# Splitting each tap of a 31-tap causal depthwise convolution on VectorE into two half-width instructions

## The reference

```python
ua, ub = jnp.split(cu, 2, axis=-1)
u = ua * jax.nn.sigmoid(ub)
u = causal_depthwise_conv(u, conv_dw_w, conv_dw_b)      # 31 taps, one filter for each channel
u = jax.nn.silu(layer_norm(u, conv_ln_g, conv_ln_b))
y_conv = u @ conv_w_proj
return (gate_a * y_gla + gate_b * y_conv) @ w_mix_out
```

## Time and profile before

| | us |
|---|---|
| median of 3 runs | 2579.86 (2576.95 to 2581.59) |
| the profiled execution | 2576.95 |
| its span, first to last instruction | 2575.2 |
| PE busy | 2496.0 (97%) |
| DVE busy | 1163.2 (45%) |
| line 1366, 240 instructions | 414.4 busy, 36.3 idle before them |

### The profile page before, as it was taken

One profiled execution on the slowest core, in us unless ns is written; L12 is line 12 of the kernel. 1 busy time (PEld: TensorE's weight loads), 2 busy tenths in 40 slices (PEclk: granted clock), 3 DMA queues, 4 the chain that ended last, 5 costly groups with the idle time before them and its releaser, 6 DMA issues. The chain is left out here.

```text
span 2575.2 us, 29372 instructions
## 1 busy us (share of the span) xinstructions
PE 2496.0 (97%) x11636; PEld 2081.1 (81%) x11636; DVE 1163.2 (45%) x1259; ACT 643.9 (25%) x823; POOL 721.7 (28%) x319
## 2 busy tenths in 40 slices
PE   7999999999999999999999986999899999999997
PEld 6888888888878889889879864888688888888886
DVE  4222222222253498598597597643622222222224
ACT  4111111111164233233333221411611111111112
POOL 2222222222262223233232273221622222222223
PEclk9999999999999999999999987999999999999999
DMA  5111111111132022132032044423511111111103
GB/s 175 50 49 49 49 49 49 49 49 49 57 123 66 25 84 60 38 99 58 25 99 74 27 162 139 159 89 114 178 50 48 44 47 45 45 49 49 49 33 114
DMA packets 189182, 184.49 MB, mean 72 GB/s; under 512 B 5813, under 2 KB 158883, under 8 KB 189091
## 3 DMA queue, kind: packets, MB, share of 16 engines
q1 hardware_dynamic: 182563, 170.67, 21.8%
q10 hardware_dynamic: 6528, 12.58, 1.3%
HBM read 150.72 MB, written 32.51 MB: 71 GB/s over the span
## 5 line engine op out<-in xcount | busy, mean ns | idle before, releaser
L442 PE MATMUL PU<-XH,w_h 128*128 128x512 f32 x2448 | 964.1, 394 | 12.2 <-POOL XL L1615 6.8
L444 PE MATMUL PU<-XH,w_l 128*128 128x512 f32 x2448 | 956.7, 391 | 0.0
L443 PE MATMUL PU<-XL,w_h 128*128 128x512 f32 x2448 | 956.5, 391 | 0.0
L1492 POOL TENSOR_TENSOR w_l<-w_raw,w_h 128x2048 fp32r<-128x2048 f32 (+1 forms) x83 | 389.9, 4697 | 1027.0 <-ACT w_h L750 1026.9
L442 PEld LDWEIGHTS PU<-XH,w_h 128*128 128x128 f32 x2448 | 462.3, 189 | 116.9 <-POOL XL L1615 11.4
L444 PEld LDWEIGHTS PU<-XH,w_l 128*128 128x128 f32 x2448 | 461.9, 189 | 96.9
L443 PEld LDWEIGHTS PU<-XL,w_h 128*128 128x128 f32 x2448 | 462.6, 189 | 95.7 <-issue 0.8
L1366 DVE SCALAR_TENSOR_TENSOR acc<-ub,cw,acc 128x1024 f32<-128x1024 f32 x240 | 414.4, 1727 | 36.3 <-DVE acc L1366 3.2
L1167 DVE TENSOR_TENSOR hf<-PU,sgt 128x512 f32<-128x512 f32 x88 | 60.8, 691 | 814.7 <-ACT sgt L817 814.7
L492 PE MATMUL PG<-o_h,H 128*128 128x512 f32 x832 | 325.5, 391 | 4.4 <-DVE FACC L1159 4.1
L493 PE MATMUL PG<-o_l,H 128*128 128x512 f32 x832 | 324.5, 390 | 0.0
(11 more groups left out here) (147 smaller groups left out, 1591.1 us busy)
## 6 DMA issues: line engine op xcount, KB each, us to landing
w_raw<-in_ffn_w_in SPq DMA_DIRECT2D x88, 512.0 KB, 5.0
w_raw<-in_w_mix_in SPq DMA_DIRECT2D x50, 512.0 KB, 5.1
o_raw<-in_ffn_w_out SPq DMA_DIRECT2D x44, 512.0 KB, 3.5
x_d<-FACC SPq DMA_DIRECT2D x16, 512.0 KB, 2.9
gate_d<-tmp ACTq DMA_DIRECT2D x16, 512.0 KB, 3.3
gt<-gate_d SPq DMA_DIRECT2D x16, 512.0 KB, 5.4
xt<-x_d SPq DMA_DIRECT2D x12, 512.0 KB, 4.2
FACC<-in_x SPq DMA_DIRECT2D x8, 512.0 KB, 6.3
```

The source lines that it names most:

```text
L442: pe.matmul(dst, hi(k), xh(k), start=(n == 0), stop=False)
L443: pe.matmul(dst, hi(k), xl(k), start=False, stop=False)
L444: last = pe.matmul(dst, lo(k), xh(k), start=False, stop=(n == KT - 1))
L1492: PT(w_l[:, par, :, c], w_raw[:, par, :, c], w_h[:, par, :, c], ALU.subtract).then_inc(w_lo, 1)
```

## The change

Each tap becomes two instructions, one for tokens 0 to 511 and one for tokens 512 to 1023 of `acc`. They alternate, and each waits not for the instruction just before it but for the one before that, which is the one that wrote its half (both halves read only `ub` beside it). There are 62 instructions in a convolution instead of 31, 61 of them count on `conv_step` and the last on `conv_free`. Nothing else changes.

```diff
-                    per = TAPS - 1
-                    o = acc[:, a, :]
+                    per = 2 * TAPS - 1
                     for w in range(TAPS):
-                        src = ub[:, a, w:w + SEQ]
-                        tap = cw[:, ds(8 * w + a + 2 * h, 1)]
-                        if w == 0:
-                            op = TS(o, src, tap, cols[:, ds(V_CB + a + 2 * h, 1)], ALU.mult, ALU.add)
-                        else:
-                            dve.wait_ge(conv_step, per * (2 * h + a) + w)
-                            op = STT(o, src, tap, o, ALU.mult, ALU.add)
-                        op.then_inc(conv_step if w < per else conv_free, 1)
+                        for half in range(2):
+                            n = 2 * w + half
+                            o = acc[:, a, half * HALF:(half + 1) * HALF]
+                            src = ub[:, a, half * HALF + w:half * HALF + w + HALF]
+                            tap = cw[:, ds(8 * w + a + 2 * h, 1)]
+                            if w == 0:
+                                op = TS(o, src, tap, cols[:, ds(V_CB + a + 2 * h, 1)], ALU.mult, ALU.add)
+                            else:
+                                dve.wait_ge(conv_step, per * (2 * h + a) + n - 1)
+                                op = STT(o, src, tap, o, ALU.mult, ALU.add)
+                            op.then_inc(conv_step if n < per else conv_free, 1)
```

## The result

The changed kernel takes 2686.61 us (median of 4 runs, 2685.11 to 2687.89) against 2580.43 for the kernel before; the ratio is 1.0411, 95% interval 1.0396 to 1.0425. That is 107 us above the forecast, and on the side of the rival "POOL is starved", to which I gave 0.05 and for which I had worked out 2760. The span of the profiled execution grew from 2575.2 to 2682.3 us, by 107.1.

The account below looks back on a forecast made before the run. PE bounds the kernel, busy 97%; DVE counts only through the last turn's two convolutions before `mean()`. There 6.2 us saved and 6.0 lost make -0.2, so 2579.7 us against the median of 2579.86; range 2572 to 2592.

Parts of the forecast that it names:

- POOL is starved: Rival, all convolutions: without gaps DVE wins every time and POOL waits for a convolution's end; +180 us, 2760; chance 0.05.
- the disturbed part: Last turn's two convolutions: 26 meetings with POOL's instructions, each costing 0.23 us more than now, 6.0 us lost.
- the rival without overlap: Rival, all convolutions: halves start only when the pipe is empty, 0.78 us each; +23.5 us, 2603; chance 0.10.
- the 25.3 us before `mean()`: PE's idle time in the last turn, waiting for DVE's chain; forecast to grow to over 30 us.
- the 0.145 us of waiting: Ahead of each dependent tap: wait and address arithmetic, said to fit in the 0.58 us since the needed half finished.
- The disturbed period: Half taps alternating with POOL's 512-element instructions: one every 1.67 us, against 2.215 for whole taps.
- Gain and loss on the last turn's chain: Last turn's two convolutions: 6.2 us saved undisturbed, 6.0 lost in meetings with POOL, together -0.2 us.
- The restart at `mean()`: Last turn: PE restarts 15.5 us after the last tap, so any shift up to 25 us earlier, or later, moves it.
- slack: First three turns: 4.9 us before PE needs DVE's work, so shorter convolutions there are worth nothing.

Follow-up runs that it names:

- experiment 2: The changed kernel, but the first half of every fourth tap waits for the half just before it, all others overlapping: 2578.2 us, ratio 0.9989.
- experiment 6: Kernel before the change with whole taps adding in turn into two accumulators, each waiting for the tap before the last, no gaps: 2668.1 us, ratio 1.0336.
- experiment 9: The changed kernel with a gap (a wait for the half just before) at every eighth tap, three in a convolution: 2583.2 us, ratio 1.0009.
- experiment 4: The changed kernel with only conv(1) of each turn in halves, conv(0) in whole taps as before: 2654.8 us, ratio 1.029.
- experiment 5: The changed kernel with a one-column DVE memset ahead of every fourth tap and no added wait: 2579.2 us, ratio 0.9998.
- experiment 8: The kernel before the change, with POOL's five layer norm additions and following low part held back until the last convolution ended: 2571.8 us, ratio 0.9958.
- experiment 1: The changed kernel, but each half waits for the half just before it, so the gap is back: 2648.2 us, ratio 1.0265.
- experiment 7: Whole taps with two accumulators, as in experiment 6, but every fourth tap waits for the tap just before it: 2572.5 us, ratio 0.9959.

## Why the prediction was wrong

**The step that failed** is the argument against the rival "POOL is starved": that POOL's instructions stand in a row without gaps and the taps get in between each two, and that "A port that lets the waiting one in that way should do so the other way too." The rows were right and the symmetry was not. In these traces DVE gets in between POOL's instructions every time. POOL gets in between DVE's only at the beginning of an unbroken row, up to the seventh instruction or 4.5 us; when it asks later, it waits for a break (experiments 2, 6, 9). The one exception is the 57th half of each conv(1) of the change. Those rows of before could not show it, since each tap had a gap ahead of it. The same error sits in "the disturbed part", which counts 26 meetings in which POOL takes its turn. The prediction says that no row has this combination, but only beside the rival without overlap; it gave starvation 0.05 on the strength of that symmetry alone.

**The rival's price** was 20 us for each conv(0) and 26 for each conv(1), four times. Measured: 23.5 for conv(0), as POOL's queue had the instruction on `ub` ahead of line 1501's; 9 to 12 for conv(1), where late address arithmetic let POOL in, and 20 to 24 where it did not (experiment 4). It left out that the 25.3 us before `mean()` would pay for a part. So its 180 us were 107.

**Right in size.** A half starts every 0.66 us (39.85 us for 60) and lasts 0.747; conv(0) takes 40.8 us (40.6); the 0.145 us of waiting fit behind the overlap. The disturbed period is 1.70 us (1.67), the conv(1) that meets POOL at its start 76.3 (76.6). Gain and loss on the last turn's chain nearly cancel where POOL is let in: from conv(0) to `mean()` experiment 2 takes 147.0 us and experiment 5 144.5, against 145.1, and both totals stand within 0.2% of the kernel before. As they have breaks or memsets that the change has not, they bear the sum out without being the kernel that it was made for.

**Right in kind.** The restart at `mean()` is the last tap's end plus a fixed way, and POOL's instructions under that convolution lengthen it by their own time (experiment 8). The convolutions of the first three turns have slack: experiment 2 shortens conv(0) by 1.1 us there, and PE has no wait less. How much a longer pair costs was not as simple as pair less slack (experiment 1).

**The two pages.** The Trainium skill's page "VectorE: DVE Perf Modes", section "The DRAIN you can't avoid", as the prediction read it, would make the half taps slower on DVE; the section also says that a next instruction that is not held starts earlier, which the prediction left out. The trace agrees with the latter: they are faster there, 40.8 us against the 43.7 worked out for whole taps. The number of instructions, which the page's rules advise to keep low, was not the reason for the loss (experiments 1 and 6). The Trainium skill's "SBUF — State Buffer", "Who interferes with whom", says that a DVE instruction with two SBUF inputs contends with a GpSimd instruction that reads SBUF, and that one with at most one, outside the modes that use two ports, does not: the memset of experiment 5 and line 1376 in experiment 9 agree. It also says that the loser blocks for the whole instruction; here it blocked for a whole row of them, 27 to 34 us.

**What stays open.** Why POOL is let in after up to 6 unbroken halves and not after 8 is not shown. The order and the times of the address arithmetic between the halves are the same in both cases. Whether the limit is a count of instructions or a time is open too: no halves asked at 7, no whole taps between 3 and 6, and no request came between 4.5 and 5.5 us. Why the late address arithmetic let POOL in is not shown either, nor whether an instruction with one SBUF input always breaks a row: tap 0 of the conv(1) behind the two of line 1376, which has one, was held up until POOL had ended, 2.47 us for 0.53.

## What to carry to other kernels

A gap on an engine can be somebody else's turn. Before a dependency stall is taken off a row of VectorE instructions with two SBUF inputs, look for GpSimd work that has to run under it, and leave a break every few instructions: here one memset of one column in every four taps cost 0.02 us each and was worth 107 us in all. And look at what the second engine's instructions do to the chain: moving six of GpSimd's from under the last convolution was worth 0.4% by itself (experiment 8), as much as the shorter convolutions were (experiment 7), and both together 0.7% to 0.8%.

## What the runs showed of the hardware

- An overlapped row of DVE instructions with two SBUF inputs held up a GpSimd instruction of 1.3 us for 32.0 us (512 elements), 27.4 (1024), and one of 2.4 us for 34.0.
- In rows without a break it got in when at most 6 of them had started before the running one (4.5 us), and after 7 or more (5.5 us or more) in no case but one: the same half of four convolutions, ahead of which DVE's address arithmetic was 0.35 us late.
- A DVE memset of 128 x 1, with no gap before or after it, let it in; so did a gap of 0.145 us, and an instruction with one input in PSUM and one in SBUF.
- Once the two alternate, they went on doing so as long as GpSimd had work queued: half taps every 1.70 us with 512-element GpSimd instructions between them, every 2.80 with 1024-element ones.
